# Grouped RMS norm of an SSM branch: pairing the squared column tiles on GpSimd before TensorE sums them

## The reference

```python
h = RMSNorm(x) * (1 + scale) + shift
proj = h @ w_in[l]                   # 1024 -> columns for all branches and gates
ya = sliding_window_attention(q, k, v) * silu(ga)
yb = multiscale_pool(u) * silu(gp)
yc = ssd_branch(z, xbc, dt)          # Mamba-2 scan
merged = g0 * (ya @ w_pa) + g1 * (yb @ w_pb) + g2 * (yc @ w_pc)
x = x + gate * (merged @ w_out[l])
```

```python
y = y.reshape(b, s, SSM_WIDTH) * jax.nn.silu(z)
y = _rms(y.reshape(b, s, SSM_GROUPS, SSM_WIDTH // SSM_GROUPS)).reshape(b, s, SSM_WIDTH)
# _rms(x) = x * rsqrt(mean(x * x, axis=-1) + EPS)
```

## Time and profile before

| what | value |
|---|---|
| median of three runs | 1238.05 us |
| profiled execution, its own time | 1237.72 us |
| its span, first to last instruction | 1235.8 us |
| mean granted TensorE clock | 0.97 of full |
| PE busy | 1155.9 us (94%) |
| POOL busy | 532.4 us (43%), 392 instructions |
| DVE busy | 602.1 us (49%) |
| ACT busy | 513.1 us (42%) |
| one L429 on POOL, mean | 1.431 us, 360 of them |

### The profile page before, as it was taken

One profiled execution on the slowest core, in us unless ns is written; L12 is line 12 of the kernel. 1 busy time (PEld: TensorE's weight loads), 2 busy tenths in 40 slices (PEclk: granted clock), 3 DMA queues, 4 the chain that ended last, 5 costly groups with the idle time before them and its releaser, 6 DMA issues.

```text
span 1235.8 us, 14931 instructions
## 1 busy us (share of the span) xinstructions
PE 1155.9 (94%) x5906; PEld 952.6 (77%) x5906; DVE 602.1 (49%) x741; ACT 513.1 (42%) x880; POOL 532.4 (43%) x392
## 2 busy tenths in 40 slices
PE   3289999999999999999989999999999999999996
PEld 2278888887888887788767888888788887778875
DVE  6754115655878633322435222565778754132434
ACT  1234334675543543322334422765454443232332
POOL 1524443444433435554533443453343425454540
PEclk9569999999999999999998999999999999999998
DMA  9824552233444233333223553332534423333321
GB/s 353 281 67 127 182 154 69 73 99 94 127 121 115 74 86 90 104 96 102 86 71 94 143 182 95 86 86 69 147 81 131 112 76 84 103 103 102 86 85 68
DMA packets 211460, 139.18 MB, mean 113 GB/s; under 512 B 11416, under 2 KB 203968, under 8 KB 209344
## 3 DMA queue, kind: packets, MB, share of 16 engines
q1 hardware_dynamic: 209968, 133.52, 37.5%
q10 hardware_dynamic: 1424, 4.72, 1.1%
HBM read 135.08 MB, written 2.62 MB: 111 GB/s over the span
## 4 chain that ended last, share of the span: by engine, by line
PE 82%; DVE 6%; DMA 5%; POOL 3%; ACT 2%; SPq 2%; issue 1%; DVEq 0%; ACTq 0%; POOLq 0%
PE main L462 72%; DMA raw<-in_w_in 4%; PE psC L462 4%; PE psA L462 3%; POOL tmp L421 1%; DVE h_lo L1238 1%; POOL w_lo L429 1%; PE psB L462 1%; DMA icnt<-in_inv_count 1%; DVE xbc L1193 1%; DVE tmp L968 1%; ACT w_hi L725 1%; DVE y_lo L1233 1%; DVE zs L1269 1%; SPq L381 1%
## 5 line engine op out<-in xcount | busy, mean ns | idle before, releaser
L429 POOL TENSOR_TENSOR w_lo<-raw,w_hi 128x512 fp32r<-128x512 f32 x360 | 507.3, 1431 | 644.8 <-ACT w_hi L725 644.8
L462 PE MATMUL main<-h_hi,w_hi 128*128 128x512 f32 x1184 | 473.1, 400 | 14.9 <-DVE h_lo L1010 5.9
L462 PE MATMUL main<-h_hi,w_lo 128*128 128x512 f32 x1184 | 463.4, 391 | 0.0
L462 PE MATMUL main<-h_lo,w_hi 128*128 128x512 f32 x1184 | 463.1, 391 | 0.0
L725 ACT ACTIVATE w_hi<-raw 128x512 fp32r<-128x512 f32 x360 | 208.4, 623 | 383.8 <-PE main L462 303.3
L462 PEld LDWEIGHTS main<-h_hi,w_hi 128*128 128x128 f32 x1184 | 223.8, 189 | 73.3 <-issue 22.0
L462 PEld LDWEIGHTS main<-h_hi,w_lo 128*128 128x128 f32 x1184 | 223.5, 189 | 48.0
L462 PEld LDWEIGHTS main<-h_lo,w_hi 128*128 128x128 f32 x1184 | 224.1, 189 | 46.5 <-issue 1.9
L1227 DVE TENSOR_TENSOR tmp<-main,misc 128x512 f32<-128x512 f32 x32 | 22.1, 691 | 201.9 <-PE main L462 201.9
L1073 DVE SCALAR_TENSOR_TENSOR misc<-main,lcol,misc 128x511 f32<-128x511 f32 (+2 forms) x96 | 71.9, 749 | 65.4 <-ACT misc L725 62.8
L462 PE MATMUL main<-y_hi,w_hi 128*128 128x512 f32 x256 | 101.6, 397 | 1.4 <-DVE y_lo L1233 1.4
(11 more groups left out here) (189 smaller groups left out, 1017.9 us busy)
## 6 DMA issues: line engine op xcount, KB each, us to landing
raw<-in_w_in SPq DMA_DIRECT2D x132, 512.0 KB, 3.8
zs<-in_w_ada SPq DMA_DIRECT2D x8, 1024.0 KB, 7.9
big<-in_w_ada SPq DMA_DIRECT2D x8, 1024.0 KB, 8.9
xbc<-in_w_ada SPq DMA_DIRECT2D x16, 512.0 KB, 4.8
raw<-in_w_pc SPq DMA_DIRECT2D x16, 512.0 KB, 3.7
raw<-in_w_out SPq DMA_DIRECT2D x16, 512.0 KB, 3.7
tmp<-step_rows SPq DMA_DIRECT2D x8, 512.0 KB, 4.2
big<-step_rows SPq DMA_DIRECT2D x8, 512.0 KB, 5.1
```

Of the source, the lines that this page charges most:

```text
L429: nc.gpsimd.tensor_tensor(w_lo[:, b, k:k + BT_, :], raw[:, b, k:k + BT_, :], w_hi[:, b, k:k + BT_, :].bitcast(F32), ALU.subtract).then_inc ...
L462: return nc.tensor.matmul(o, a, b_, start=start, stop=stop)
```

## The change

GpSimd gets one new instruction in each mix stage: it waits for ACT's squares and adds, for each of the four groups, the second squared tile to the first, in place (128x512 elements). TensorE waits for this sum, not for the squares, and makes four products in place of eight. The new instruction stands on POOL behind the split of (u+2, 1) and ahead of that of the next stage.

```diff
@@ gpsimd, mix section, at the end of each stage p
                     for m in range(2):
                         split(l, u + 1 + m, 0)
                         split(l, u + 1 + m, 1, BT_)
+                    pool.wait_ge(s_ysq, l * PAIRS + p + 1)
+                    sq = buf_x.rearrange("p (g t n) -> p g t n", t=2, n=PAIR)
+                    nc.gpsimd.tensor_tensor(sq[:, :, 0], sq[:, :, 0], sq[:, :, 1], ALU.add).then_inc(s_ysum, 1)
                 section(l, U_B, KT, BT_)
@@ tensor
             def norm_mm(l, p):
-                pe.wait_ge(s_ysq, l * PAIRS + p + 1)
+                pe.wait_ge(s_ysum, l * PAIRS + p + 1)
                 for g in range(SG):
-                    for t in range(2):
-                        last = mm(psC1[:, g * P:(g + 1) * P], ones[:, 0:1].broadcast_to([P, P]),
-                                  buf_x[:, (2 * g + t) * P:(2 * g + t + 1) * P], t == 0, t == 1)
+                    last = mm(psC1[:, g * P:(g + 1) * P], ones[:, 0:1].broadcast_to([P, P]),
+                              buf_x[:, 2 * g * P:(2 * g + 1) * P])
                 last.then_inc(s_yn, 1)
```

More of the change, by code:

```diff
@@ L228, in build @@
         s_yo, s_st, s_stu = sem("y_off"), sem("states"), sem("state_updated")
-        s_yd, s_yu, s_yz, s_ysq = sem("y_diag"), sem("y_combined"), sem("y_gated"), sem("y_squared")
+        s_yd, s_yu, s_yz, s_ysq, s_ysum = (sem(n) for n in ("y_diag", "y_combined", "y_gated", "y_squared",
+                                                            "y_squares_paired"))
         s_yn, s_y = sem("y_norm_product"), sem("y_normed")
```

## The result

The changed kernel took 1247.94 us (median of five runs, 1245.43 to 1251.84). The kernel before took 1238.05 us beside it (1236.46 to 1238.12). The ratio is 1.0087, with a 95% interval of 1.0073 to 1.0101. So the change costs some 10 us where +2.4 was forecast, and the time lies outside of the range of 1236.2 to 1243.0. The runs spread over 6.4 us, those of before over 1.7. (A ratio given here need not be the exact quotient of the two medians.)

The account below looks back on a forecast made before the run. PE was taken as the bound, except in p = 0 to 2, where y_hi, y_lo, two scans and POOL's split make it wait. The sum -0.84 x 2 + 0.68 x 6 = +2.4 gave 1240.4 us, range 1236.2 to 1243.0.

Parts of the forecast that it names:

- Removed from PE: Half the norm products go: 0.84 us less per stage, gained in two p = 3 stages, turned into wait in six.
- Added to POOL: One 128x512 add per stage, 1.30 us, done 0.32 us before PE wants the sum, so no cost on PE.
- What the add pushes: In p = 0 to 2 DVE's y_lo, the scans and POOL's split come 0.68 us later; price 4.1 us over six.
- the upper end: Largest y_lo shift considered, 0.83 us, if y_lo needs its whole 0.69 us behind the add; price 5.0 us.
- The wait on PE: PE's idle time ahead of h_tile(u+3, 0) grows from 0.44 to 1.96 us in six places.
- the clock falls: Rival, 4%: longer PE waits lower the granted clock, each fall costing up to 5 us; 5 to 30 above 1240.4.
- The hidden add: Rival, 12%: DVE isn't held or raw's landing sets the split's end; two stages give 0.84 us each, 1236.4 us.
- PE as the bound everywhere: Rival, 3%: all eight stages pass on their gain, 6.7 us in all, giving 1231.3 us.
- The long add: Rival, 13%: POOL's add takes 2.46 us, not 1.30, shifting y_lo, scans and split by 1.84 us; 1249 us.

Follow-up runs that it names:

- experiment 2: The change with norm_mm's four products made twice (16 instructions, as before): 1242.95 us against 1238.53 for the kernel before, ratio 1.0036.
- experiment 1: The change plus eight unread extra products on PE during its wait in p = 0 to 2: 1243.30 us against 1238.53 for the kernel before.
- 6: The kernel before with four products, no add, and PE waiting for both halves of w_lo: 1248.96 us against 1237.84, ratio 1.0089.
- 9: The change with its four products made twice and PE waiting for both halves of w_lo: 1252.84 us against 1238.21 for the kernel before.
- 8: The change with DVE's second scan behind L1136 and raw of u+3 issued earlier: 1229.71 us, -8.1 against the kernel before, ratio 0.9934.

## Why the prediction was wrong

Its sum was right, term by term, and stopped short of one.

*Removed from PE: right.* From norm_mm to the next block it is 0.81 us (363.06 to 363.87) in place of 1.70, so 0.89 less and not 0.84. In p = 0 to 2 all of it was turned into wait; in p = 3 the first tile of U_B starts 3.64 us behind norm_mm (446.14 against 442.50), where it was 4.54.

*Added to POOL: right.* The add took 1.29 us, 1.30 forecast, and ended at 362.71, before PE wanted the sum (363.06). PE never waited for it.

*What the add pushes: right.* y_lo took 1.37 us in all eight stages, as said, and ended 0.55 us behind the add (363.26 against 362.71), as the row of L1211 had it. (The full 0.69 us behind the add would have shifted it by 0.84, not by the 0.83 of the upper end.) The stages are longer by 0.66 and 0.69 us where the clock stayed up, which makes 4.1 in all; experiment 2 measures this share alone as +4.4.

*The wait on PE: right in size, wrong in price.* It was forecast as 1.96 us and came as 1.85 to 2.00. The step that failed is that the sum put nothing for the granted clock over six waits of 1.96 us and gave the rival "the clock falls" 4%. I argued that a wait of 1.74 us had left the clock at 1.00 and took 1.96 for the same kind. The runs show otherwise: in the mix sections the clock fell in 13 of 24 places with 1.85 us or more, and in none of 54 with 1.72 or less. The row itself was a lucky draw: the same wait at the layers' ends had a fall in 11 of 26 places, in the changed kernel's profile too. A fall in a mix stage costs 1.58 us, not the "up to 5" that I took from the start of layer 1. Four of them and one at the layer's end are 7.8 of the 10.3 us. That it is PE's idle time is shown from three sides: filling it takes the falls away (1, 2), making it in another way brings them without the add (6), and the number of products doesn't matter (9). A fall that comes only in some places also fits the spread of the runs: their mean granted clock goes from 0.965 in the fastest (1245.43) to 0.959 in the slowest (1251.84).

*The rivals.* The hidden add and PE as the bound everywhere are both out; the second became true in the mix sections only when the scan and raw were moved (8). The long add is out too, at 1.29 us in all eight stages.

*Left open.* It isn't known why one place has a fall and its twin in the other layer hasn't, nor whether the length of the one wait decides or how much PE idles in a longer stretch around it; the waits outside of the mix sections speak against the length alone. The falls at the layers' ends stand in 9 of the 13 profiles, and in those of experiment 1 lies a part of the difference from its forecast.

## What to carry to other kernels

Before taking work from an engine, look at what ends its next wait: six of eight savings here only lengthened one. Then ask what the longer wait does to TensorE's clock, since a saving of 0.89 us cost 1.58 where the clock fell, and don't take one profile in which the clock stayed up for a bound: look at several places and runs. A POOL instruction is not free on an idle POOL if DVE's next one has two inputs in SBUF and stands on the path (y_lo went from 0.69 to 1.37 us here): look for what waits for that. Where a scan of 2.3 us stands ahead of a split for which PE waits, change their order first; then the saving begins to count (3.0 us here, and 5.9 with raw issued earlier too).

## What was unexpected in the hardware

The granted clock fell after single waits of 1.85 to 2.45 us in the midst of sections in which PE is otherwise at work without a stop (busy for 114.3 of 120.1 us), in 13 of 24 such places, and in none of 54 places with up to 1.72 us. At the layers' ends, where a wait of 0.53 us comes just before, 1.75 us was followed by a fall in 11 of 26 places of otherwise equal code. A kernel with 16 useless matmul instructions in each of six stages stood 4.8 us above the kernel before; the same kernel without them stood 9.9 us and, measured again on another chip, 13.1 us above it.
